# Four slots for the high parts of the weights, split three beats ahead; the sample queries' buffer in a shared home

## The reference, cut to what matters

```python
h = rms_norm(x, norm_g)
proj = h @ w_in                       # 2048 -> 13,840 columns
(a_q, a_k, a_v, a_z, b_u, b_z, c_q, c_k, c_v, c_lr, c_z, gates) = split(proj)
q = rope(rms_norm(a_q, q_norm_g), pos);  k = rope(rms_norm(a_k, k_norm_g), pos)
o_a = sink_attention(q, k, a_v, ...)  # exp(s - max), a learned sink in the sum
o_b = multiscale_pool(b_u, ...)       # trailing means over 2, 4, 8, 16
o_c = rms_norm(gla(c_q, c_k, c_v, log_sigmoid(c_lr @ w_gate_lr + b_gate) / 16))
branches = [o_a * silu(a_z), o_b * silu(b_z), o_c * silu(c_z)]
br = einsum('blnc,ncd->blnd', branches, w_branch)
merged = sum(sigmoid(gates) * br)
y = x + merged @ w_out
```

## Time and profile before

| | us |
|---|---|
| three runs | 2300.32, 2300.53, 2301.46 |
| median | 2300.53 |
| the profiled execution's own time | 2300.78 |
| its span | 2299.0 |
| PE busy | 2282.6 (99% of the span) |
| weight loads (PEld) busy | 2236.1 (97%) |
| DVE busy | 1371.7 (60%) |
| ACT busy | 1014.1 (44%) |
| GpSimd (POOL) busy | 70.8 (3%) |

### The profile page before, as it was taken

How to read it: one execution, slowest core, us unless ns; L and a number is a source line. 1 busy time by engine, 2 the same in 40 slices (tenths; PEclk the granted TensorE clock), 3 DMA queues, 4 the chain that set the end, 5 groups by cost and what they waited for, 6 DMA issues and landing times.

```text
span 2299.0 us, 40263 instructions
## 1 busy us (share of the span) xinstructions
PE 2282.6 (99%) x16664; PEld 2236.1 (97%) x16664; DVE 1371.7 (60%) x2350; ACT 1014.1 (44%) x1816; POOL 70.8 (3%) x108
## 2 busy tenths in 40 slices
PE   9999999999999999999999999999999999999999
PEld 9999999899999999999999999988999999999999
DVE  6767757765455455456657778578654555455443
ACT  5444356754333333333344443566533333333332
POOL 0100100000000000000001001000000000000000
PEclk9999999999999999999999999999999999999999
DMA  7443653334444444445554436533344444444454
GB/s 279 145 152 130 229 184 119 104 117 154 147 149 154 147 148 153 149 148 197 191 208 137 150 128 237 181 116 105 120 150 153 147 149 154 147 150 153 148 195 154
DMA packets 97559, 360.79 MB, mean 157 GB/s; under 512 B 11408, under 2 KB 11664, under 8 KB 96544
## 3 DMA queue, kind: packets, MB, share of 16 engines
q1 hardware_dynamic: 86976, 314.48, 41.2%
q0 software_dynamic: 9680, 42.36, 5.2%
q10 hardware_dynamic: 720, 1.36, 0.2%
HBM read 341.59 MB, written 20.50 MB: 158 GB/s over the span
## 4 chain that ended last, share of the span: by engine, by line
PE 91%; DVE 5%; ACT 3%; issue 1%; DMA 0%; ACTq 0%; DVEq 0%
PE main L1550 85%; PE side L1550 5%; DVE w_lo L444 1%; PE side L1554 1%; ACT tc L1307 1%; ACT w_hi L1099 1%; ACT probs L1267 0%; DVE small L811 0%; DVE q_a L459 0%; DVE probs L806 0%; DVE tc L459 0%; ACT tb L1119 0%; DVE ta L463 0%; DVE ta L513 0%; DVE q_a L783 0%
## 5 line engine op out<-in xcount | busy, mean ns | idle before, releaser
L444 DVE TENSOR_TENSOR w_lo<-raw,w_hi 128x512 fp32r<-128x512 f32 x1192 | 791.9, 697 | 526.6 <-ACT w_hi L1099 520.9
L1550 PE MATMUL main<-xg_hi,w_hi 128*128 128x320 f32 x3488 | 1092.9, 313 | 1.0 <-DVE w_lo L444 0.9
L1550 PE MATMUL main<-xg_hi,w_lo 128*128 128x320 f32 x3488 | 1077.7, 309 | 0.0
L1550 PE MATMUL main<-xg_lo,w_hi 128*128 128x320 f32 x3488 | 1077.6, 309 | 0.0
L1099 ACT ACTIVATE w_hi<-raw 128x512 fp32r<-128x512 f32 x1192 | 715.2, 626 | 701.6 <-PE main L1550 679.9
L1550 PEld LDWEIGHTS main<-xg_hi,w_hi 128*128 128x128 f32 x3488 | 654.8, 188 | 10.7 <-issue 3.4
L1550 PEld LDWEIGHTS main<-xg_lo,w_hi 128*128 128x128 f32 x3488 | 655.1, 188 | 1.9
L1550 PEld LDWEIGHTS main<-xg_hi,w_lo 128*128 128x128 f32 x3488 | 654.8, 188 | 0.0
L1550 PE MATMUL main<-branch_hi,w_hi 128*128 128x320 f32 x768 | 237.3, 309 | 0.0
L1550 PE MATMUL main<-branch_lo,w_hi 128*128 128x320 f32 x768 | 237.3, 309 | 0.0
L1550 PE MATMUL main<-branch_hi,w_lo 128*128 128x320 f32 x768 | 237.3, 309 | 0.0
(11 more groups left out here) (234 smaller groups left out, 1296.0 us busy)
## 6 DMA issues: line engine op xcount, KB each, us to landing
raw<-in_w_stream SPq DMA_DIRECT2D x595, 512.0 KB, 3.3
state<-in_state POOLq DMA_DIRECT2D x16, 512.0 KB, 6.2
out_state_s<-state POOLq DMA_DIRECT2D x16, 512.0 KB, 3.0
w_pool<-in_w_pool POOLq DMA_DIRECT2D x2, 1024.0 KB, 7.9
cache_k<-in_cache_k POOLq DMA_DIRECT2D x2, 1024.0 KB, 5.0
cache_v<-in_cache_v POOLq DMA_DIRECT2D x2, 1024.0 KB, 7.0
out_k_window<-in_cache_k_tok POOLq DMA_DIRECT2D x2, 960.0 KB, 10.1
out_new_v_s<-in_cache_v_tok POOLq DMA_DIRECT2D x2, 960.0 KB, 11.7
```

The costliest lines, as they stand in the source:

```text
L444: dve.tensor_tensor(w_lo[Q % RAWS][:, half], raw[Q % RAWS][:, half], w_hi[Q % HIS][:, half].bitcast(F32), ALU.subtract).then_inc(lo_ready, 1)
L1550: return pe.matmul(out, lhsT, rhs, start=start, stop=stop)
```

## The change

There are four slots for w_hi in place of three. Every call of `split_hi_to` and `split_lo_to` in the input, mix and output phases goes three beats ahead in place of two, and stands at the head of its beat; the second call in beats with scores is gone on both engines. `q_s` moves to a home that it shares with tiles of branch C (behind `cache_v`), and since these overwrite it, it is zeroed in each layer, at beat 73 after PE's step `sample_gla` 7, no longer at beat 10.

```diff
-RAWS, HIS = 5, 3
+RAWS, HIS, AHEAD = 5, 4, 3
...
-        q_s = place("q_s", [P, 2, NB, 2, 4, TS])
...
+        q_s = place("q_s", [P, 2, NB, 2, 4, TS], at=part_a + 16384)
...
+                    v.mark("masks", 0, 0)
+                if beat == 73:
+                    wait_step(l, "sample_gla", 7)
                     v(dve.memset(q_s[:, :, :, :, :, :].rearrange("p i b j g t -> p (i b j g t)"), 0.0))
-                    v.mark("masks", 0, 0)
+                    v.settle()
...
-                        split_lo_to(Q0 + 6 * n + part + 2)
+                        split_lo_to(Q0 + 6 * n + part + AHEAD)
...
-                    split_lo_to(Q0 + part + 2)
+                    split_lo_to(Q0 + part + AHEAD)
...
                     vector_probs(l, beat)
-                    split_lo_to(Q + 2)
+                    split_lo_to(Q + AHEAD)
                     vector_softmax(l, beat)
-                    if scored_at(beat):
-                        split_lo_to(Q + 3)
                     vector_part(l, beat)
...
-                        split_hi_to(Q0 + 6 * n + part + 2)
+                        split_hi_to(Q0 + 6 * n + part + AHEAD)
...
-                    split_hi_to(Q + 2)
-                    if scored_at(beat):
-                        split_hi_to(Q + 3)
+                    split_hi_to(Q + AHEAD)
                     scalar_part(l, beat)
...
-                    split_hi_to(Q0 + b + 2)
+                    split_hi_to(Q0 + b + AHEAD)
```

## The result

The changed kernel took 2308.07 us in the median of seven runs (2306.76 to 2310.44), the kernel before 2300.6 beside it (2300.32 to 2304.73). The ratio is 1.0031, with a 95% interval of 1.0022 to 1.0041: slower, by 5 to 9 us. Forecast were 2306.5 and slower. The profiled execution took 2307.05 with a span of 2305.3, 6.3 more than before; forecast for it were 5.9.

The account below looks back on a forecast made before the run. PE, busy 99% of the span, was taken as the bound, so only its waits move. 5.32 + 1.21 - 0.60 = +5.93 us on 2300.78 gave 2306.7, put at 2306.5 beside the median; 8-in-10 range 2298.5 to 2309.5.

Parts of the forecast that it names:

- ACT in the periods: Attention, beats 82 to 101: a w_hi pair between exponentials and inverse root adds 1.04 us, period 18.93 to 19.97.
- DVE at the softmax: Attention: w_lo pair moves from behind maximum to ahead of mask; nothing in three periods, 1.21 us saved at beat 93.
- What follows: Later attention steps: `p_turn` 4 is 2.18 us late in all, `p_turn` 6 waits 0.48; 2.66 per layer, +5.32 for both.
- The start: First beats: one more DVE pair affects the sum of squares that PE takes, +1.21 us, once.
- The softplus: Turn from beat 12 to 13: block 13 is split before the softplus on ACT, -0.60 us for two layers.
- The zeroing: `q_s` on DVE, 0.91 us, moved to beat 73 and done twice: 0; if not covered, up to 0.9 a layer.
- mix and output phases: ACT's split result comes one beat earlier than wanted; PE has no wait to lose there: 0.
- The raw ring: Five raw slots stay; blocks land just within a beat and ACT may wait: counted 0, up to 2 us in range.
- rival C: Beats 82 to 101 and start: late blocks hold ACT; signs PE waiting for w_lo, ACT for DMA; 2310.5, chance 0.13.
- A, faster: Attention: DVE's moved pair shortens four long waits a layer, the pair on ACT costs nothing; 2291.5 us, chance 0.13.
- B: No change: attention's pair on ACT is hidden or taken back later; 2301.1, or 2298.7 with `p_turn` 3's gain; chance 0.12.
- D: Periods of attention: four slots and three ahead need not lengthen lookahead where ACT is late; no size or chance of its own.

## Why the prediction was right, point by point

**ACT in the periods.** Right in the place and nearly in the size. A pair of 1.04 us stands between exponentials and root, the period is 19.87 where I had 19.97, `p_turn` 1 and 2 lose 0.93 each where I had 1.04. Putting the pair elsewhere between exponentials and swaps leaves the period at 19.86, so it is ACT's sum of work that counts; I had reasoned by the root, which DVE waits for, and by ACT's lack of idle time. The first is not needed, the second is. The traces bear it out half by half: what the change adds to the period, 0.93, lies between exponentials and swaps, and nothing between the swaps and the next exponentials. A kernel with DVE's new order and ACT's old one was not run, so the split into an ACT part and a DVE part rests on these halves.

**DVE at the softmax.** Right in the number by luck, wrong in what moves and in the reason. I had a pair go from behind the maximum to ahead of the mask. In the periods it goes to the head of the next beat, ahead of the normed queries, and one pair stands ahead of the mask in both kernels. It costs nothing in its new place because the queries are ready at 366.22 + 0.88 = 367.10 and ACT starts the swaps, behind its own work, only at 367.70. My reason was another: DVE had waited ahead of the mask for ACT anyway (1.40 and 2.50 us), as if that idle time were cover. It was the chain itself: taking the wait and the pair away at either place gave 9 to 11 us. A pair really put ahead of the mask would by this have cost its length. The change left these waits nearly as they were (1.40 and 2.25 after), which is why the sum came out. The one part that the change does take off, at beat 93, is there: beats 95 and 96 together -0.17, forecast 1.91 - 2.08 = -0.17.

**What follows.** Beat 97 +0.18 (forecast 0.27), beat 101 +0.85 (forecast 0.48, inside its bounds of 0 and 1.21). The 0.85 goes with DVE's order alone: it is gone in both layers with DVE's old order in attention and stays with the pair ahead of the mask moved, though the periods are as short there. Beats 84 to 101 cost 2.8 a layer, forecast 2.66; in both layers alike. Two errors of size nearly cancel in this: the two periods cost 0.2 less than forecast, beat 101 0.4 more.

**The start.** +1.20 at beat 5, forecast 1.21. What I did not see is that taking it back would gain only about half, because the first take is next.

**The softplus.** -0.30 in each layer, as forecast. **The zeroing, mix and output phases.** 0, as forecast.

**The raw ring.** ACT waits 718.8 us for blocks, where before it waited for PE; PE gained or lost nothing by it, also not at beat 6 of layer 1 (-0.09 at beat 5, +0.08 at beat 6). Neither of rival C's signs is there: ACT waits for no block and PE for no low part in beats 82 to 101.

**The sum.** Forecast +5.93, measured in the span +6.3. The median of the runs moved by 7.5. The least run of each kernel (2306.76 and 2300.32) differ by 6.4, as the profiles do. For the remainder I take the half-clock stretches, which the forecast had no term for: the steps between runs are of their size, but only the traced executions show them.

**The rivals.** A, faster, had the right place (the rows name DVE's probabilities, and both waits for ACT lie on the way to them). More slots and one more block of lookahead took away none of the ten gaps; that its 2291.5 is near the 2290.62 of the version with DVE one behind is a coincidence, since that version gains by taking out DVE's waits for ACT, which A did not name. B and D: with the order in attention taken back the ratio is 1.0004, so four slots and the extra block of lookahead are worth nothing in sum where both engines have it and attention keeps its order.

**A slip in the text.** The second listing of orders ahead of the prediction is said to be of beats 86 and 87; its rows are those of beats 92 and 93 (step 3 of the softmax). At beat 86 the rotary product stands ahead of the mask, as the timelines show, and no second pair comes to stand ahead of the mask. The sum is not touched, as it used the pair behind the maximum at beat 93 alone.

## What to carry to other kernels

Here two engines prepare an operand one after the other. A deeper buffer with both moved ahead alike brought nothing or a loss (ratios 1.0004 and 1.0031): the second still waited for the first at the same heads. With the first one block further ahead than the second it gave 0.9952. It is worth trying where one engine's work feeds another's; that it must hold elsewhere is not shown. And idle time of an engine is cover only if nothing on the chain is queued behind it: a wait followed by two operations and then by a chain operation is part of the chain, although the engine is 60% busy and the wait is booked to a high part of a weight. Look at what starts right after the wait and who waits for that.

## What the runs showed of the hardware

TensorE's granted clock fell to half for some 3.4 us in beat 11 of a layer in some executions and not in others, in kernels with the same work there. The windows view (stretch, us, busy PE, PEld, DVE, ACT, POOL, clock, DMA, GB/s) of the run with DVE's old order in attention, and of the one with DVE one behind everywhere:

```profile
51.80:55.20 3.40, 3.40 (x14) 3.35 (x14) 1.93 (x4) 1.27 (x1) 0.00 (x0) 0.52 1.30 545
```

```profile
50.50:55.00 4.50, 4.50 (x28) 3.95 (x27) 3.22 (x6) 1.47 (x2) 0.07 (x1) 1.00 1.09 444
```

PE starts 14 matmuls in 3.4 us in the first; with a mean of 0.52 of full speed nearly all of the stretch is at the lower of the two levels, 1.2 GHz. The beat takes 5.16 us in place of 3.62, so one such stretch costs 1.5. Ahead of it PE ran the small matmuls of the gate (16 rows), in all executions alike:

```profile
51.23 0.70 PE L1577 MATMUL side<-ta,w_gate 16*128 16x320 f32 x2
51.86 0.60 PE L1577 MATMUL main<-xg_hi,w_hi 128*128 128x320 f32 x1
52.26 0.47 PE L1577 MATMUL main<-xg_lo,w_hi 128*128 128x320 f32 x1
```

It was in beat 11 of layer 0, of layer 1, of both or of none: six of the eleven traces have at least one. A seventh, of the kernel with the pair ahead of the rotary product moved, has its stretch in beat 97 of layer 0, with PE idle for 1.78 of the 3.98 us ahead of it:

```profile
418.00:421.98 3.98, 2.20 (x22) 1.79 (x21) 2.64 (x5) 3.70 (x5) 0.00 (x0) 1.00 0.39 132
421.98:425.39 3.41, 3.41 (x15) 3.41 (x14) 2.89 (x10) 2.18 (x10) 0.00 (x0) 0.50 0.00 0
```

There it cost nothing: beats 96 and 97 together changed by 1.08 us in this layer and by 1.07 in the other, which had no such stretch. In layer 1 PE waits 1.6 us for probabilities behind the matmuls of beat 97; in layer 0 this wait is gone and the slow matmuls stand in its place. So what a stretch costs depends on whether PE waits behind it anyway. The runs of one kernel lie in steps accordingly (of the kernel with the pair behind the root: 2306.15 to 2306.35 three times, 2307.71 to 2308.10 three times, 2309.72 to 2309.94 three times). That the steps of the untraced runs are these stretches is inferred from their size. Why it falls there in some executions only was not tried. For a kernel like this one it means that medians of few runs are uncertain by 1.5 us, and that a difference of 1 us is read from the beats of two traces.
